# Work order at the stage heads of a three-block float32 kernel: product order in first pairs, early sums, evictions among bias steps, and no barrier before the delta rule

## The reference

```python
def first_block(x, ...):              # two layers
    h = rmsnorm(x, norm_g[0]); branch, gate = split(h @ s5_w_in)
    y = gelu(s5_mixer(branch, ...))   # complex diagonal state, chunks of 64
    y = y * sigmoid(y @ s5_w_glu + s5_b_glu)
    x = x + (y * silu(gate)) @ s5_w_out
    h = rmsnorm(x, norm_g[1]); u, v, gate = split(h @ sgu_w_in)
    y = gelu(u) * (W_s @ layernorm(gelu(v)) + b_s)    # 128-token blocks, 8 heads
    x = x + (y * silu(gate)) @ sgu_w_out
    return rmsnorm(x, final_g)
def second_block(x, p, ...):
    h = layer_norm(x); proj = h @ w_in
    o_gdn = gated delta rule on q, k, v of proj, chunks of 64; o_fox = forgetting attention
    h = layer_norm(ALPHA * h + concat(o_gdn, o_fox) @ w_out)
    ff = square(relu(h @ w_up)) @ w_down
    ple = (p @ w_ple) * sigmoid(h @ w_ple_gate + b_ple_gate)
    return layer_norm(ALPHA * h + ff + ple)
def third_block(x, ...):              # three gated linear mixers, one output product
    return rmsnorm(x + mixers(rmsnorm(x)) @ w_out)
```

## Time and profile before

| | |
|---|---|
| runs | 4239.3, 4246.41, 4247.28 us; median 4246.41 us |
| profiled execution | 4236.57 us, span 4234.8 us |
| mean granted TensorE clock | 0.963 |
| PE busy | 3921.8 us, 93% |
| DVE busy | 1733.1 us, 41% |
| ACT busy | 892.4 us, 21% |
| POOL busy | 561.8 us, 13% |

### The profile page before, as it was taken

One profiled execution on the slowest core, in us unless ns is written; L12 is line 12 of the kernel. 1 busy time (PEld: TensorE's weight loads), 2 busy tenths in 40 slices (PEclk: granted clock), 3 DMA queues, 4 the chain that ended last, 5 costly groups with the idle time before them and its releaser, 6 DMA issues.

```text
span 4234.8 us, 32236 instructions
## 1 busy us (share of the span) xinstructions
PE 3921.8 (93%) x12911; PEld 1986.7 (47%) x12911; DVE 1733.1 (41%) x2510; ACT 892.4 (21%) x1031; POOL 561.8 (13%) x609
## 2 busy tenths in 40 slices
PE   5999999999898999977979999999899999899997
PEld 3455344444344776444434444444345554444553
DVE  6576433433433543144343333323444544324423
ACT  2112111110362211243120000000142430221122
POOL 0143210121000321022111212212000000000000
PEclk8999999999999999999989999999999999999998
DMA  3233111111011110200021111111101101003101
GB/s 110 78 72 93 35 50 41 40 48 42 15 35 36 31 36 21 70 21 21 10 60 40 40 50 40 50 40 41 39 25 26 30 11 40 18 13 97 30 13 42
DMA packets 291106, 174.50 MB, mean 41 GB/s; under 512 B 24096, under 2 KB 281999, under 8 KB 290703
## 3 DMA queue, kind: packets, MB, share of 16 engines
q1 hardware_dynamic: 253008, 126.47, 11.0%
q0 software_dynamic: 10000, 24.39, 2.2%
q10 hardware_dynamic: 27950, 21.58, 1.7%
HBM read 159.20 MB, written 13.21 MB: 41 GB/s over the span
## 4 chain that ended last, share of the span: by engine, by line
PE 53%; DVE 3%; ACT 2%; issue 1%; DMA 0%; POOL 0%; ACTq 0%; DVEq 0%
PE products L308 22%; PE products L2825 8%; PE products L161 7%; PE products L2838 3%; PE others L2904 2%; PE products L2028 1%; PE products L179 1%; PE products L500 1%; PE products L2191 1%; PE others L2222 1%; PE products L2037 1%; PE products L3353 1%; PE products L3352 1%; PE others L1441 1%; PE others L2937 1%
## 5 line engine op out<-in xcount | busy, mean ns | idle before, releaser
L161 PE MATMUL products<-normed,weights 128*128 128x512 f32 x704 | 314.9, 608 | 30.2 <-ACT work L2467 23.3
L2825 PE MATMUL products<-normed,weights 128*128 128x512 f32 (+2 forms) x704 | 317.9, 601 | 5.0 <-DVE normed L486 5.0
L308 PE MATMUL products<-gate,s_small 128*128 128x512 f32 x704 | 313.2, 592 | 0.0
L308 PE MATMUL products<-work,s_small 128*128 128x512 f32 x544 | 247.8, 599 | 11.9 <-DVE work L228 7.5
L326 POOL TENSOR_TENSOR s_small<-weights 128x512 f32<-128x512 f32 x60 | 78.1, 1302 | 1192.6 <-PE products L308 1010.5
L308 PE MATMUL products<-normed,s_small 128*128 128x512 f32 x512 | 230.9, 593 | 0.7 <-DVE normed L228 0.7
L161 PEld LDWEIGHTS products<-normed,weights 128*128 128x128 f32 x704 | 135.9, 195 | 201.5 <-issue 166.6
L308 PE MATMUL products<-normed,weights 128*128 128x512 f32 x448 | 208.0, 608 | 10.7 <-ACT s_small L338 6.4
L338 ACT ACTIVATE s_small<-products 128x512 f32<-128x512 f32 x60 | 35.9, 598 | 861.3 <-PE products L308 861.3
L308 PEld LDWEIGHTS products<-gate,s_small 128*128 128x128 f32 x704 | 133.8, 190 | 168.4 <-issue 168.1
L2825 PEld LDWEIGHTS products<-normed,weights 128*128 128x128 f32 (+2 forms) x704 | 125.1, 184 | 161.7 <-issue 159.7
(11 more groups left out here) (566 smaller groups left out, 6145.4 us busy)
## 6 DMA issues: line engine op xcount, KB each, us to landing
weights<-in_w_in_dram SPq DMA_DIRECT2D x83, 512.0 KB, 3.9
weights<-in_w_up_dram SPq DMA_DIRECT2D x32, 512.0 KB, 4.9
weights<-in_w_down_dram SPq DMA_DIRECT2D x32, 512.0 KB, 4.7
weights<-in_sgu_w_in_dram SPq DMA_DIRECT2D x24, 512.0 KB, 5.1
weights<-in_s_w_in_dram SPq DMA_DIRECT2D x16, 512.0 KB, 3.9
weights<-in_w_out_dram SPq DMA_DIRECT2D x24, 256.0 KB, 2.7
work<-in_x_dram ACTq DMA_DIRECT2D x8, 512.0 KB, 9.7
branch_scratch<-work POOLq DMA_DIRECT2D x8, 512.0 KB, 2.9
```

Source lines behind the costliest of these rows:

```text
L161: last = pe.matmul(out[0:cols, half * BANK:(half + 1) * BANK], slot(c, b, kt, cols)[:, k, :], acts[n][:, half * BANK:(half + 1) * BANK], s ...
L308: last = pe.matmul(bank, w[:, k * P:(k + 1) * P], moving[k], start=(k == 0 and n in (1, 3, 5)), stop=(k == KT // 2 - 1), skip_group_check= ...
L2825: last = pe.matmul(out[0:cols, half * BANK:(half + 1) * BANK], slot(c, f.b, kt, cols)[:, kk, :], acts[kk][:, half * BANK:(half + 1) * BANK ...
```

## The change

- `Split.make` makes one T sum and signals it by itself; `Ready` holds the order of the signals. In `sgu`, `s5_gate`, `mix` and `ff` the T sums are made in new orders: T1 for all k ahead of the others, or T3 and T4 at different places.
- A pair with such waits (the first of each kind in a stage) runs its products in the order 1, 5, 3, 2, 4, 6, 7. There are ten.
- `add_all` takes two more steps: the collection of tile 2i - 1 ahead of `u3` and that of tile 2i ahead of `c12`. The last tile is collected by nobody: `mean_of_total` adds it by two more matmuls into the same banks.
- S5 gate: the weight sums of the first pair are made by GpSimd ahead of the last store of the scan's result; the gating of the upper four tiles comes behind the T sums.
- Spatial gating: ScalarE copies product 1 of the first pair ahead of the last root steps, VectorE does `u2` and T4 between the last two normalisations, and the gating of tile a is cut in two halves, the first ahead of tile b.
- Delta rule: no barrier ahead of it; 18 quanta run behind the products of k and q, ahead of `turn`, in place of 8 behind it; ten later points with 3 quanta have 2.
- Feed-forward: ScalarE evicts embedding group k behind bias step k of the layer norm; `aside` comes behind the first gate pair.

```diff
-    ORDER = (1, 3, 2, 4, 5, 6, 7)
+    ORDER, FIRST = (1, 3, 2, 4, 5, 6, 7), (1, 5, 3, 2, 4, 6, 7)
+        self.order = self.FIRST if self.ready else self.ORDER
...
-    def add_all(self, dve, a, b, scale=None):
+    def add_all(self, dve, a, b, scale=None, early=None, late=None):
         self.add(dve, b[:, lo], self.c.pair_t, scale)
+        if early is not None:
+            early()
         self.u3(dve)
         self.add(dve, b[:, hi], self.c.pair_v, scale)
         self.c22(dve, b[:, hi], b[:, hi])
         self.c21(dve, b[:, lo], b[:, lo])
+        if late is not None:
+            late()
         self.c12(dve, a[:, hi], a[:, hi])
...
+    tile, sem, value = sums.last
+    pe.wait_ge(c.collected, sums.collected + KT - 2)
     for h in range(HALVES):
+        pe.matmul(out[:, h * BANK:(h + 1) * BANK], c.mean_mat[:, :], sums.total[:, h * BANK:(h + 1) * BANK],
+                  start=True, stop=False)
+    pe.wait_ge(sem, value)
+    for h in range(HALVES):
+        last = pe.matmul(out[:, h * BANK:(h + 1) * BANK], c.mean_mat[:, :], tile[:, h * BANK:(h + 1) * BANK],
+                         start=False, stop=True)
...
             act.activation(dst[:, k, :], dst[:, k, :], ACT.Identity, bias=bias[:, k:k + 1]).then_inc(c.normed, 1)
+            phase.between(act, k)
...  s5_scan_phase, gpsimd
+            if i == S5_C - 1:
+                phase.cover(pool)
             pool.wait_ge(c.s5_y_read, i + 1)
...  s5_gate_phase, vector
         for k in range(HALF):
-            gated(HALF + k)
+            ys.make(c, dve, "T1", k, y_ready)
+        for k in range(HALF):
+            dve.wait_ge(c.s5_y_gelu, HALF + k + 1)
             if k == 2:
                 dve.wait_ge(c.s5_y_stored, 16 * S5_T * S5_C)
-            ys.first(c, dve, k, c.pair_ready)
-            ys.second(c, dve, k, c.pair_ready)
+            for name in SUMS[1:]:
+                ys.make(c, dve, name, k, y_ready)
+        for m in range(HALF, KT):
+            gated(m)
...  residual_sums
-        for m in (2 * i - 2, 2 * i - 1):
-            if m >= 1:
-                sums.collect(dve, m)
-    for m in (KT - 2, KT - 1):
-        sums.collect(dve, m)
+        pair.add_all(dve, sums.src[:, 2 * i + 1, :], sums.src[:, 2 * i, :], scale,
+                     *((lambda m=2 * i - 1: sums.collect(dve, m), lambda m=2 * i: sums.collect(dve, m)) if i else ()))
...  sgu_phase, scalar and vector
+            if n == len(g_v) - 1:
+                us[0].copy(act)
...
             for i in (first, first + 1):
+                if final and i > first:
+                    us[0].u2(dve)
+                    for k in range(HALF):
+                        hs.make(c, dve, "T4", k, h_ready)
...
+            dve.wait_ge(c.pair_c11, pair.evicted)
+            ch.done(dve.tensor_tensor(mixed[a][:, 0:T], mixed[a][:, 0:T], blocks(stage[:, 0, lo]), ALU.mult))
...  gdn_phase
-    quota = []
+    quota = [18]
-        quota += [(8 if it == 0 else 0) if few else 8, 2] + [1 if few else 2] * (LEVELS - 1) + [2 if few else 3] * 6
+        quota += [0 if few else 8, 2] + [1 if few else 2] * (LEVELS - 1) + [3 if it == 2 and n < 2 else 2 for n in range(6)]
...
         products(0), products(1)
+        advance()
         turn(0), turn(1)
...  ff_phase
+    def take_ple(act, m):
+        act.activation(c.D[:, m, :], take_group(c, act, g_ple + m), ACT.Copy).then_inc(c.group_read[(g_ple + m) % 2], 1)
+    norm.between = take_ple
-        aside.scalar(act)
-        for m in range(KT):
-            act.activation(c.D[:, m, :], take_group(c, act, g_ple + m), ACT.Copy).then_inc(c.group_read[(g_ple + m) % 2], 1)
...
+            if i == 0:
+                aside.scalar(act)
...
-        then(gdn_input_phase(c, t, norm.normed), meet=True)
+        then(gdn_input_phase(c, t, norm.normed))
```

More of the change, by code:

```diff
@@ L221, in __init__, with make, signalled, at @@
         self.part = {"B11": self.B11, "B21": self.B21, "B22": self.B22, "T1": self.T1, "T2": self.T2, "T3": self.T3, "T4": self.T4}
-    def first(self, c, dve, k, signal):
+    def make(self, c, dve, name, k, ready):
         ch = c.dve_chain
+        ready.signalled(name, k)
         ch.wait()
[L226 to L241, removed]
+        if name == "T1":
+            ch.done(dve.tensor_tensor(self.T1[k], self.B12[k], self.B11[k], ALU.subtract), c.pair_ready)
+        elif name == "T2":
+            ch.done(dve.tensor_tensor(self.T2[k], self.B22[k], self.T1[k], ALU.subtract), c.pair_ready)
+        elif name == "T3":
+            ch.done(dve.tensor_tensor(self.T3[k], self.B22[k], self.B12[k], ALU.subtract), c.pair_ready)
+        else:
+            ch.done(dve.tensor_tensor(self.T4[k], self.B21[k], self.T2[k], ALU.subtract), c.pair_ready)
+SUMS = ("T1", "T2", "T3", "T4")
+class Ready:
+    def __init__(self, c, names):
+        self.first, self.names, self.next, self.sem = c.n_pair_ready, list(names), 0, c.pair_ready
+        c.n_pair_ready += len(self.names)
+    def signalled(self, name, k):
+        assert self.names[self.next] == (name, k), (self.names[self.next], name, k)
+        self.next += 1
+    def at(self, name, k):
+        return self.sem, self.first + self.names.index((name, k)) + 1
+    def needs(self, start=None):
+        need = {(name, k): self.at(name, k) for name in SUMS for k in range(KT // 2)}
+        if start is not None:
+            for k in range(KT // 2):
                 need["B11", k] = start(k)
@@ L475, in tensor @@
         if sums is not None:
[L476 removed]
+            mean_of_total(c, pe, g, sums)
             return
@@ L1141, in tensor @@
             pair.tensor(pe)
+    scan.cover = units[0].pool
     def gpsimd(pool):
-        for pair in units + outs:
+        for pair in units[1:] + outs:
             pair.pool(pool)
@@ L2360, in mix_phase @@
     xs = Split(tiles, parts(c.Bt, 2), parts(c.Bt, 3), parts(c.Ct, 0))
-    ready = c.n_pair_ready
-    c.n_pair_ready += 2 * HALF
+    ready = Ready(c, [(name, k) for name in SUMS for k in range(HALF)])
     pairs = []
@@ L2400, in mix_phase @@
     means = Means(c, c.X)
+    means.ends_with(pairs[-1].g + 1)
     def vector(dve):
-        for k in range(HALF):
-            xs.first(c, dve, k, c.pair_ready)
-        for k in range(HALF):
-            xs.second(c, dve, k, c.pair_ready)
-        for i, pair in enumerate(pairs):
-            pair.add_all(dve, c.X[:, 2 * i + 1, :], c.X[:, 2 * i, :], ALPHA)
-            for m in (2 * i, 2 * i + 1):
-                if m:
-                    means.collect(dve, m)
+        for name in SUMS:
+            for k in range(HALF):
+                xs.make(c, dve, name, k, ready)
+        residual_sums(c, dve, pairs, means, ALPHA)
     phase = Phase(tensor=tensor, scalar=scalar, vector=vector, gpsimd=gpsimd, loads=loads)
@@ L2415, in mix_phase, with ff_phase @@
     return phase
-def ff_phase(c, t, normed, aside):
+def ff_phase(c, t, norm, aside):
     QUARTERS, HALF = 4, KT // 2
@@ L2433, in ff_phase @@
     x = Split(inner, parts(c.W2, 0), parts(c.W2, 1), parts(c.W2, 2))
-    ready = c.n_pair_ready
+    normed = norm.normed
+    h_ready = Ready(c, [("T1", k) for k in range(HALF)] + [(name, k) for k in range(HALF) for name in SUMS[1:]])
+    x_ready = [Ready(c, [(name, k) for k in range(HALF) for name in ("B",) + SUMS]) for _ in range(QUARTERS)]
     gates, pairs = [], []
@@ L2492, in vector @@
         for k in range(HALF):
+            dve.wait_ge(c.normed, normed + k + 1)
+            h.make(c, dve, "T1", k, h_ready)
+        for k in range(HALF):
             dve.wait_ge(c.normed, normed + k + HALF + 1)
-            h.first(c, dve, k, c.pair_ready)
-            h.second(c, dve, k, c.pair_ready)
-        aside.vector(dve)
+            for name in SUMS[1:]:
+                h.make(c, dve, name, k, h_ready)
         for m in range(2):
@@ L3799, in build @@
         then(s5_input_phase(c, t, norm.normed))
-        then(s5_scan_phase(c, t))
-        gate = then(s5_gate_phase(c, t))
+        scan = then(s5_scan_phase(c, t))
+        gate = then(s5_gate_phase(c, t, scan))
         norm = then(rms_phase(c, c.X, c.B, c.vec["norm_g1"], sums=gate.sums))
```

103 lines of the change are left out of this document (53 added, 50 removed).

## The result

The changed kernel takes 4184.11 us (median of 4 runs, 4178.53 to 4190.77) against 4245.84 us for the kernel before in the same comparison (4 runs): ratio 0.9858, 95% interval 0.9840 to 0.9876, 61.7 us less. A second comparison gave 4188.12 (4 runs) against 4242.22 (9 runs), 0.9878 (0.9861 to 0.9895), 54.1 us less. The forecast was 4177 with 4157 to 4200. The profiled execution took 4190.77 us, 6.7 over its median, and that of before (4236.57 us) lay 9.3 under the median given here, so those two profiles differ by 45.8 us only; the fifth group of experiments shows where the rest is.

What follows compares the result with a forecast made beforehand. TensorE, busy 93% of the span, was taken as the bound. 24.1 - 5.2 + 19.1 + 13.6 + 7.4 + 8.6 + 2.1 = 69.7 us off the median 4246.4 gave 4177 us, range 4157 to 4200.

Steps and rivals of the forecast that it cites:

- Means: Norm ends of several stages: earlier mean matmuls and faster squares stages, less 1.6 us lost at load; 19.1 us saved.
- order gap: Ten pairs in the new product order: product 6 waits 1.0 us for `u3`; six pairs outside the heads sum to -5.2.
- mixing head: Start of the mixing stage: first pair takes 27.7 us in place of 29.8; 2.1 us saved, bounds 0 and 3.
- feed-forward head: Feed-forward start: interleaved evictions start the first gate pair 26.1 us earlier; 24.1 us saved after `aside` and the gap.
- S5 gate head: First S5 gate pair: 12.4 us earlier, less 3.8 for four VectorE instructions slowed beside GpSimd; 8.6 us, bounds 7 and 12.4.
- Delta rule: Delta-rule start and later points: chain starts 5 us earlier, ten quanta fewer save 8.6; 13.6 us, bounds 5 and 16.
- Gating head: First gating pair: products 6 and 7 end 7.4 us earlier, including a 2.0 us wait before product 6; bounds 5 and 9.4.
- Rival (a): Slow records follow each of the ten stops between products 4 and 6: 30 us lost, 4207 us; chance 0.06.
- rival (b): TensorE stops at each embedding group, half of 24 us lost; missing delta-rule quanta uncover VectorE, 8.6 lost: 4198 us, chance 0.09.
- (d): In the delta rule the clock falls to the lower level from 1364 to 1500 us, +115: 4292 us; chance 0.02.
- (c): More gain than counted, from S5 sums, squares stages, the delta-rule chain start and unseen waits: 4162 us, chance 0.11.
- my own signs of a wrong forecast: Feed-forward head gives under 20 us, or the clock in the ten pairs or the delta rule is below 1.0.

Runs made afterwards that it cites:

- the fifth group of experiments: The changed kernel and the kernel before, each run once more unchanged for a second profile; also the changed kernel with five edits together, 4155.79 us, ratio 0.9805 to before.
- the second profiles: Profiles from running the changed kernel and the kernel before once more, each unchanged; medians in that comparison 4188.12 and 4242.22 us.

## Why the prediction was right, and where not

The time and most terms came as worked out. **Means** (12.2 for 12.3, 6.3 for 6.4, load +1.1 for +1.6), **order gap** (0.83 us of idleness, 1.07 to 1.08 in the pairs where it was taken out; I said 1.0), **mixing head** (1.8 for 2.1) and **feed-forward head** (26.2 for 26.1) need no other story. Squares stages gave 2.8 for 2.0.

**S5 gate head, "Four of the six are hit: 4 x 0.95 = 3.8 us later".** This step failed: the pair started 9.1 us later. Two things were missing. Four instructions were hit, but one of them was a scan, which lost 1.8 us where an addition loses 0.9 to 1.0; from the start of the scans to the last addition VectorE took 11.4 us in place of 6.8, 4.6 us more. In the two executions where the scan was missed the 3.8 us came out as worked out. And TensorE, waiting for VectorE, came back at the lower of its two clock levels (two records of 128x128 in 0.79 in place of 0.49 us), so that ScalarE waited 4.20 us for its y products; this term, which I had not put down at all, made the other 4.5 us. The Trainium skill's rule cited in the forecast, in the page "SBUF — State Buffer", section "SBUF: two separate sides", gave 5.2 us for VectorE's part, and the trace's 4.6 is nearer to that than to my 3.8; no execution showed more than 4.7. My bounds for the part (7 and 12.4) did not hold the 2.8, nor the 0.9 between the second profiles.

**Delta rule.** The step of ten quanta at 0.86 us held; the part measured 11.9 between the first and 9.2 between the second profiles, for 13.6. I ascribed nothing to the barrier, and it is worth 0.2. Not foreseen was the 5.18 us for the first mask with 16 slow records behind it: I let the chain start when `turn` and `kd` were done, and it waits for a longer VectorE sequence and then GpSimd. The kernel before showed this wait already, in its second iteration, which had none of the eight quanta there:

```profile
1446.85 4.04 PE L1903 MATMUL others<-work 128*128 128x128 f32 x16 [5.18 <-POOL work L1837]
```

**Gating head.** The stop before product 6 was 2.4 us (I said 2.0); what I left to the bound, slow records behind it, came in this execution, as in six of nine others, and cost 1.7. Without them the part is 6.8, for 7.4.

**Feed-forward head: right number, incomplete cause.** I put the 23.27 us down to the bias steps. ScalarE's own waits in the trace of before show 13.94 of them behind `aside`. The number came out right because either cause is removed by the interleaving; in that it was luck.

**What the size missed as a whole.** The sum was 9.5 us too large by the first profiles, 5.8 of it in the S5 head, and about 15 by the second. Rival (a) did not happen: nine of the ten stops had no slow records behind them. Of rival (b) nothing was seen, since the embedding groups ran without a stop, and (d) did not happen: the stage got shorter. Two slips of arithmetic changed little: the six pairs of the order item add up to 5.3, not 5.2, and the terms of (c) as written to 17.6 to 19.6 us, so its time is 4157 to 4159, not 4162. By my own signs of a wrong forecast one came true, a clock below 1.0 in the ten pairs or in the delta rule: product 6 of the gating pair had a granted clock of 0.68 over its 5.37 us, and the delta rule 0.97 over its 338.9 us. The sign was badly chosen, since the delta rule of the kernel before had 0.95, and the cost behind it was 1.7 us in the gating pair.

## What to carry to other kernels

Work of a second engine that is moved into that engine's idleness needs a place where the engine it slows is idle too: here four sums cost 9 us beside a scan and its additions, 6 us beside the sums of the next stage, and nothing in the 7 us between, when VectorE had nothing to do. When a stop is ended by an engine, read that engine's own wait too; the releaser (an eviction) was itself behind a tiny computation that stood behind sixteen sums. And before two profiles are compared stage by stage, read one stage that the change left alone: here it differed by 11 us.

## What the runs showed of the hardware

A VectorE scan of 128x512 took 1.20 us alone and 2.9 to 3.1 us beside GpSimd, and an addition of 128x508 0.69 and 1.57 to 1.72 us; GpSimd's four sums of 128x512 took 1.26 to 1.30 us alone and up to 2.08 us there. Beside the four sums four VectorE instructions were slowed, in nine executions of nine. The same stop of 2.4 us was followed by 8 records in 5.19 to 5.37 us (seven executions) or in 3.67 us (three). A stage of unchanged instructions took 232.6 to 243.8 us, with granted clocks of 0.92 to 0.88.
